# Where the sums of a modulation row stand in TensorE's order, in a two-block transformer kernel

## The reference, cut to what matters

```python
sh, sc, gt = jnp.split(jax.nn.silu(c) @ w_ada[l] + b_ada[l], 3, axis=-1)
sh_c, sc_c, gt_c = jnp.split(jax.nn.silu(c_ctx) @ w_ada[l] + b_ada[l], 3, axis=-1)
h = rms_norm(x, norm_g[l]) * (1 + sc[:, None]) + sh[:, None]
hc = rms_norm(ctx, norm_g[l]) * (1 + sc_c) + sh_c
qa, ka, va, ga, qb, kb, vb, gb, qn, kn, vn, gn = split_proj(h @ w_in[l])
...
x = x + gt[:, None] * y
```

## Time and profile before

| | us |
|---|---|
| median of three runs | 1298.64 (1297.81 to 1301.27) |
| the profiled execution | 1296.14 |
| its span | 1294.4 |
| TensorE busy | 1150.7 (89% of the span) |
| VectorE busy | 727.3 (56%) |
| ScalarE busy | 601.9 (47%) |
| GpSimd busy | 250.4 (19%) |

### The profile page before, as it was taken

The page is one execution under the profiler, slowest core; times in us unless marked ns, Lnnn a source line. Parts: engine busy times, 40 slices in busy tenths (PEclk is TensorE's granted clock), DMA queues, the critical chain, the costliest instruction groups (busy, mean ns, idle before and its releaser), DMA issues.

```text
span 1294.4 us, 16688 instructions
## 1 busy us (share of the span) xinstructions
PE 1150.7 (89%) x5877; PEld 910.5 (70%) x5877; DVE 727.3 (56%) x1320; ACT 601.9 (47%) x1174; POOL 250.4 (19%) x324
## 2 busy tenths in 40 slices
PE   4787879899987977989989798998889999999987
PEld 0475557677675866668867686887668888888875
DVE  0448677786763554464444656565465655565543
ACT  0443335444662353454464553444444445445553
POOL 4146060326004104112300204000012211121100
PEclk9798889898997999889989999998999999999999
DMA  8626344333203123213110664553446565434301
GB/s 232 230 89 198 104 136 131 113 115 84 96 2 102 66 82 113 65 53 95 66 49 26 235 217 145 179 177 128 136 155 187 179 185 172 126 118 117 129 1 49
DMA packets 79001, 157.92 MB, mean 122 GB/s; under 512 B 5760, under 2 KB 6056, under 8 KB 78664
## 3 DMA queue, kind: packets, MB, share of 16 engines
q1 hardware_dynamic: 75592, 147.41, 36.2%
q0 software_dynamic: 3328, 9.46, 2.9%
HBM read 153.73 MB, written 3.11 MB: 121 GB/s over the span
## 4 chain that ended last, share of the span: by engine, by line
PE 69%; DVE 10%; ACT 8%; issue 5%; POOL 4%; SPq 2%; DMA 2%; ACTq 0%; POOLq 0%; DVEq 0%
PE bank L665 16%; PE bank L667 16%; PE bank L666 16%; PE bank L803 5%; PE bank L778 3%; PE bank L788 3%; PE bank L878 2%; POOL small L1398 2%; ACT w_hi L977 2%; DVE w_lo L1537 2%; DVE work L1557 2%; PE bank L851 2%; SPq L562 2%; PE bank L863 2%; PE bank L685 1%
## 5 line engine op out<-in xcount | busy, mean ns | idle before, releaser
L665 PE MATMUL bank<-w_lo,h_hi 128*128 128x512 f32 (+1 forms) x1152 | 461.5, 401 | 33.5 <-DVE h_lo L1605 16.7
L666 PE MATMUL bank<-w_hi,h_lo 128*128 128x512 f32 (+1 forms) x1152 | 446.6, 388 | 0.0
L667 PE MATMUL bank<-w_hi,h_hi 128*128 128x512 f32 (+1 forms) x1152 | 446.5, 388 | 0.0
L1537 DVE TENSOR_TENSOR w_lo<-raw,w_hi 128x1024 fp32r<-128x1024 f32 x224 | 285.9, 1282 | 280.9 <-ACT w_hi L977 279.4
L977 ACT ACTIVATE w_hi<-raw 128x1024 fp32r<-128x1024 f32 x224 | 235.8, 1057 | 294.1 <-PE bank L667 249.9
L665 PEld LDWEIGHTS bank<-w_lo,h_hi 128*128 128x128 f32 x1152 | 222.5, 193 | 84.0 <-issue 38.9
L667 PEld LDWEIGHTS bank<-w_hi,h_hi 128*128 128x128 f32 x1152 | 221.6, 192 | 44.9
L666 PEld LDWEIGHTS bank<-w_hi,h_lo 128*128 128x128 f32 x1152 | 223.0, 194 | 40.0 <-issue 0.2
L803 PE MATMUL bank<-work,stage 128*128 128x128 f32 x640 | 94.8, 291 | 1.5 <-ACT stage L1164 1.3
L1155 ACT ACTIVATE stage<-bank,small 128x512 f32<-128x512 f32 (+1 forms) x96 | 56.9, 596 | 71.1 <-DVE small L1752 71.0
L803 PEld LDWEIGHTS bank<-work,stage 128*128 128x128 f32 x640 | 85.2, 204 | 3.3 <-ACT stage L1164 2.7
(11 more groups left out here) (166 smaller groups left out, 1102.3 us busy)
## 6 DMA issues: line engine op xcount, KB each, us to landing
raw<-in_b_w_in_dram SPq DMA_DIRECT2D x80, 512.0 KB, 3.6
raw<-in_w_in_dram SPq DMA_DIRECT2D x56, 512.0 KB, 3.7
raw<-in_a_w_in_dram SPq DMA_DIRECT2D x48, 512.0 KB, 4.0
raw<-in_w_ada_dram SPq DMA_DIRECT2D x32, 512.0 KB, 3.7
work<-in_w_ada_dram SPq DMA_DIRECT2D x16, 512.0 KB, 13.9
raw<-in_w_out_dram SPq DMA_DIRECT2D x16, 512.0 KB, 3.5
raw<-in_a_w_out_dram SPq DMA_DIRECT2D x16, 512.0 KB, 3.5
raw<-in_b_w_out_dram SPq DMA_DIRECT2D x8, 512.0 KB, 3.5
```

Source lines behind the costliest of these rows:

```text
L665: pe.matmul(bank, hT(h_hi, ph, kt, tt), w_lo[:, s, k, lo:lo + w], start=first, stop=False)
L666: pe.matmul(bank, hT(h_lo, ph, kt, tt), w_hi[:, s, k, lo:lo + w], start=False, stop=False)
L667: mm = pe.matmul(bank, hT(h_hi, ph, kt, tt), w_hi[:, s, k, lo:lo + w], start=False, stop=last)
L1537: dve.tensor_tensor(w_lo[:, i % SPLIT, :, :], raw[:, PIECE_AT[p] % RAW, :, :], w_hi[:, i % SPLIT, :, :].bitcast(F32), ALU.subtract).then_i ...
```

## The change

The call of `ada_total` moves from the end of a piece, behind all its products, into its loops: behind the six matmuls of the first token tile where the tiles are outside, and behind the second tile of the first half in `by_half`. Only TensorE's function changes.

```diff
@@ -713,12 +713,12 @@
                             for tt in tts:
                                 for k in range(2):
                                     product(ph, c, p, k, tt)
+                                if tt == 0 and p in ADA_READY:
+                                    ada_total(*ADA_READY[p])
                                 if tt % 2 and c and (n, tt // 2) in TURNED_AFTER:
                                     head_turn(ph, c - 1, TURNED_AFTER[(n, tt // 2)])
                         else:
                             by_half(ph, c, p, n, after_piece)
-                        if p in ADA_READY:
-                            ada_total(*ADA_READY[p])
                         if after_piece:
                             after_piece((p, 1))
                     for tt in tts if ending else ():
@@ -740,6 +740,8 @@
                 for k in range(2):
                     for tt in tts:
                         product(ph, c, p, k, tt)
+                        if (k, tt) == (0, 1) and p in ADA_READY:
+                            ada_total(*ADA_READY[p])
                     tt = TURNED_AFTER.get((n, k))
                     if c and tt in tts:
                         head_turn(ph, c - 1, tt)
```

## The result

The changed kernel took 1303.28 us in the median of 20 runs (1299.42 to 1307.23), the kernel before, beside it, 1300.68 us (20 runs). The ratio is 1.0026 with a 95% interval of 1.0014 to 1.0037: about 3.4 us slower by the ratio (the medians lie 2.6 us apart). That is just inside the 0.3% named as the bound, and the upper end of the interval is outside. The profiled execution has a span of 1300.6 us, against 1294.4. Not all of these 6.2 us belong to the change. The head turn of piece (1,3), ahead of the first moved sum, already comes at 120.08 in place of 118.86.

The account below looks back on a forecast made before the run. TensorE was taken to hold 69% of the chain, so only shifts in its stream or awaited hops count. Terms 1.4 + 0 + 1.8 + 0 + 0 = +3.2 us on 1298.64 gave 1301.9 us, range 1297.5 to 1306.0.

Parts of the forecast that it names:

- Which calls move; VectorE's list is the crux: Projection "in0": five sums move past 18 matmuls; VectorE's untouched list keeps each sum only behind the split, after w_hi and w_lo.
- (2,0): Piece of chunk 2, pair 0: TensorE waits for VectorE's last row product, delaying the first attention step, +1.4 us.
- (3,0): Piece of chunk 3, pair 0: about 1 us wait for OUT_BANK, hidden in the 6.83 us idle before the turn, 0.
- a sign of being wrong: Turns of (3,0) and (5,0): idle before them shrinking by more than is spent at the sum's new place.
- (4,0): Piece of chunk 4, pair 0: the early sum delays products, w_hi, w_lo, kept sum and turn, +1.8 us.
- (5,0): Piece of chunk 5, pair 0: w_hi shifts 1.8 us but still ends well ahead of w_lo, 0.
- (6,0): Piece of chunk 6, pair 0: VectorE's 0.35 us wait goes, TensorE's scores end as before, 0, at best -0.3 us.
- The sum: Terms of the five pieces added, 1.4 + 0 + 1.8 + 0 + 0 = +3.2 us; forecast's chance 0.50.
- Rival A: At (4,0) the new idle makes the granted clock fall to 0.5: +5.4 in all, 1304.0 us, chance 0.22.
- Rival B: One or both terms vanish behind another late engine or transfer: 1300.4 or 1298.6 us, chance 0.19.
- Rival C: L788's waits really end on the sum, so 11.4 us go: 1287.2 us, chance 0.09.

Follow-up runs that it names:

- run 11: The changed kernel measured once more against the kernel before: ratio 1.0040 (1.0022 to 1.0058).
- run 7: The changed kernel with `ada_keep` ahead of `split_until` in VectorE's list, still behind the head norms: ratio 0.9968 against the kernel before.
- run 8: The changed kernel with `ada_keep` first in the piece, ahead of the head norms too; sums early: ratio 0.9959 against the kernel before.
- run 9: The kernel before, sums late, with `ada_keep` first in the piece: ratio 0.9960 against the kernel before.
- run 10: As run 8, but sums of (2,0) and (3,0) behind tile 1 instead of tile 0: ratio 0.9949 against the kernel before, median 1293.79 us.
- run 3: The kernel before with only the sum of (2,0) early, behind token tile 1: 19.90 us from head turn to restart of the first attention step.
- run 12: Run 7 measured once more: ratio 0.9983 (0.9965 to 1.0001) against the kernel before.
- run 5: The kernel before with only the sum of (4,0) early and its matmuls issued twice: 16.43 us turn to turn at (4,0).
- run 6: The kernel before, sums late, with the matmuls of the sum of (4,0) issued twice: 11.02 us turn to turn at (4,0).
- run 1: The kernel before with only the sum of (2,0) early, behind tile 0: 21.19 us to the restart, 9.63 us at (4,0).
- run 4: The kernel before with only the sums of (3,0), (5,0) and (6,0) early: ratio 1.0007 (0.9986 to 1.0028).

## Why the prediction was right, by its own steps

**The time.** 1301.9 us were forecast (1298.64 + 3.2 is 1301.84, so rather 1301.8), 1303.28 measured. The 1.4 us between them are the base and not the change: over 20 runs the kernel before has a median of 1300.68, 2.0 us above the three runs that the forecast started from. The forecast took about 0.3% as what can be told from no change. Twenty runs told 0.26% from none, but that the result lies below 0.3% is partly luck: the repeat (run 11) gave 0.40%.

**Which calls move; VectorE's list is the crux.** Right. The turns still wait for the kept sums, and runs 7 to 10 show that it is the place of `ada_keep` that decides.

**(2,0), +1.4: measured +1.2.** The mechanism is right, and run 3 takes it away. The term is slightly oversized, because VectorE's products ended 2.95 us after the head turn (120.16 + 2.87 - 120.08), against 3.20 before. In the kernel before the first of them had waited 0.26 us for its transfer, here it waited for none. In runs 8 and 12 it did (0.29 and 0.23 us), the products ended 3.25 and 3.18 us after the head turn, and the stretch was 21.37 and 21.30. So the stretch follows the end of the products at a distance of 18.1 us. With the 3.20 us of the kernel before it would have been 21.3, the forecast's +1.4, and the term lies between 1.2 and 1.5 us with the landing of one transfer.

**(3,0), 0: +0.02.** The wait for OUT_BANK is 0.83 us against 1.0 forecast, and the turn's idle 5.70 against 5.8. Taken by the letter, a sign of being wrong did appear: the idle shrank by 1.13 us, by more than the 0.83 spent at the new place. But the turn came no earlier (16.65 against 16.63). The other 0.3 us are TensorE being busy a little longer, which the idle time swallows.

**(4,0), +1.8: +1.86.** L979, L1539, L1567 and the turn stand in the forecast order and distances, and runs 5 and 6 bound the sum's length and its cover. The idle before the turn is 2.00 us against 1.8.

**(5,0), 0: 0.** Right. The idle before the turn shrank by 0.17 us (4.25 to 4.08) with nothing spent at the new place. That is the small price of (6,0) below, hidden here.

**(6,0), 0, at best -0.3: +0.17.** VectorE's wait went and TensorE didn't see it, as forecast. But a small price was missed. The seven traces with a late sum of (6,0) have 8.99 to 9.02 us in this stretch, the seven with an early one 9.15 to 9.17. A part of it can be seen, and (4,0) has it too: the first projection matmul behind a sum takes longer. The chain of the changed kernel at (4,0) (start us, us, what):

```profile
209.87 1.68 PE bank L622 x16
211.55 0.35 PE bank L665
```

0.35 us in place of 0.23. With the sum at the end of these pieces the scores stood behind it, and the step from a sum to a projection did not occur. The remaining 0.05 us have no place in the trace.

**The sum, +3.2: +3.3 by the stretches,** and 3.4 by the ratio. That the ratio agrees so closely is luck, as its interval is some 3 us wide.

**Rival A, the clock.** It did not come about: in the changed kernel the granted clock behind the turn of (4,0) is 1.00. It is the kernels with the *late* sum that can lose the clock there. The step behind that turn, first of the changed kernel, then of run 1, whose sum of (4,0) stands late:

```profile
218.43:226.00 7.57, 7.57 (x40) 5.99 (x41) 3.95 (x10) 2.38 (x8) 0.00 (x0) 1.00 0.51 141
```

```profile
217.17:226.33 9.16, 9.16 (x40) 7.37 (x40) 4.19 (x10) 2.38 (x8) 0.00 (x0) 0.81 0.51 173
```

Of the six traces with a late sum at (4,0), four took 9.16 to 9.21 us at a mean of 0.81 (runs 1, 4, 6 and 9), the kernel before and run 3 took 7.6 at 1.00. All eight with an early one took 7.55 to 7.59 at 1.00. So the early sum seems to save 1.6 us behind (4,0) in some executions. The prediction did not see that, and the table does not hold it, as its trace of before is one without the fall. How often that happens was not measured, and the ratio shows no net gain.

A standstill of 2.00 us cost no clock here. The page of the Trainium skill named in the prediction, "TensorE: Matmul & The Clock Gate", section "Part 1: The HAM clock gate (the "warmup" mystery)", ties the lower rate to idling. The low stretches behind the idle times of 5.47, 6.83 and 4.25 us agree with it. Those behind the late sum do not, since TensorE had stood still for 0.33 us or less just before them, and run 5 does not either, as told below.

**Rival B, swallowed.** Both terms appear in full, and the next idle time (5.47 us in either kernel) took nothing of the first. **Rival C, faster.** It fell with the 5.70, 2.00 and 4.08 us that remain. What it hoped for can be had, but from VectorE's list: runs 8 to 10 remove these waits, and by their ratios 5.2 to 6.6 of the 11.4 us are left of it.

## What to carry to other kernels

When an engine waits for "the result of X", look at what stands ahead of X's consumer in its list, before moving X. Here the sum was never late; its keeper stood behind a step that needs the end of the very piece that the early sum delays. A piece of work placed behind the last product may run under a chain that this product starts, and moved ahead of it, it delays that chain by its own length. Small moves are best read from stretches between fixed instructions within one execution: those of the table repeated to 0.1 us, or followed a landing transfer, where totals scatter by several us. Look at the granted clock as well: steps of TensorE without a wait differed by up to 1.6 us with nothing changed in them, by how long the clock was low.

## What the runs showed of the hardware that was not expected

The granted clock fell in run 5 while the profile had TensorE busy without a gap: 4.20 us busy of 4.20 at a mean of 0.80, then 5.00 of 5.00 at 0.50. What it did there, from 205.87 to 210.31, were 32 matmul records with a single column each. This made the doubled sum dearer in front of long products than its own length tells: 3.1 us, beside 1.8 us for the added matmuls. In the seven traces with a single early sum (16 records) the clock stayed at 1.00 through the piece.

Behind a late sum it can fall too, at a single length as well as doubled. In run 9 TensorE was busy without a gap from 206.00 to 212.79, the products, the sum and the scores, all at 1.00, and then had 4.21 us busy of 4.21 at a mean of 0.59. It fell behind the single late sums of runs 1 and 4 too, while the kernel before and run 3, with the same order of TensorE in this piece, stayed at 1.00. In the other direction, the standstill of 2.00 us before the turn of (4,0) cost nothing in any of the four traces that have it. But one of 1.39 us before a head turn was followed by 0.57 from 260.50 to 264.50 in run 10, and by no fall in run 8. So idle time in the profile's sense does not alone decide when the clock comes down. What does was not tested.
